# A fused attention and pooling block on one Trainium2 core: x^T laid out by the host, rows of x queued behind the weights, K's chain of round 0 two halves later

## The reference

```python
h = x * rsqrt(mean(x * x, axis=-1) + 1e-6) * norm_w
q, k, v, g_a, u_p, g_p = split(h @ w_in)              # six times 1024 columns
q, k = rope(rms_norm(q, q_norm_w)), rope(rms_norm(k, k_norm_w))   # by head of 64
a = softmax(q1 k1^T / 8) - lam * softmax(q2 k2^T / 8)  # 8 heads of 2 x 64
attn = rms_norm(a @ v) * subln_w * (1 - 0.2)
pool = (centred_mean(u_p, w) - u_p) @ w_pool * pool_scale   # w = 2, 4, 8, 16
out = x + concat(attn * silu(g_a), pool * silu(g_p)) @ w_out
```

## Time and profile before

| | us |
|---|---|
| median of 3 runs | 796.71 (796.64 to 797.11) |
| the profiled execution | 798.08 |
| its span, first to last instruction | 796.3 |
| PE busy | 780.4 (98%) |
| DVE busy | 550.3 (69%) |
| ACT busy | 389.6 (49%) |
| POOL busy | 31.3 (4%) |
| HBM read | 90.98 MB |
| mean granted TensorE clock | 1.000 |

### The profile page before, as it was taken

One profiled execution on the slowest core, in us unless ns is written; L12 is line 12 of the kernel. 1 busy time (PEld: TensorE's weight loads), 2 busy tenths in 40 slices (PEclk: granted clock), 3 DMA queues, 4 the chain that ended last, 5 costly groups with the idle time before them and its releaser, 6 DMA issues.

```text
span 796.3 us, 9964 instructions
## 1 busy us (share of the span) xinstructions
PE 780.4 (98%) x3522; PEld 643.5 (81%) x3522; DVE 550.3 (69%) x825; ACT 389.6 (49%) x647; POOL 31.3 (4%) x42
## 2 busy tenths in 40 slices
PE   6999999999999999999999999999999999999998
PEld 5888788888887888888878888887888878888886
DVE  3668775862786767637967674398667788777796
ACT  4945455444354644435436433544455556555552
POOL 0010000000000000000000000000000020233100
PEclk9999999999999999999999999999999999999999
DMA  9524521223244222232532123236222599999912
GB/s 319 170 81 133 158 80 54 80 79 106 85 130 132 78 80 79 75 111 85 144 113 79 53 79 97 88 105 182 79 64 72 164 246 296 327 250 211 196 54 105
DMA packets 69439, 101.87 MB, mean 128 GB/s; under 512 B 5152, under 2 KB 55584, under 8 KB 69408
## 3 DMA queue, kind: packets, MB, share of 16 engines
q1 hardware_dynamic: 62656, 82.52, 32.7%
q0 software_dynamic: 4736, 16.78, 10.8%
q10 hardware_dynamic: 2016, 2.18, 1.0%
HBM read 90.98 MB, written 4.19 MB: 120 GB/s over the span
## 4 chain that ended last, share of the span: by engine, by line
PE 81%; DVE 7%; ACT 5%; issue 3%; DMA 3%; SPq 0%; DVEq 0%; ACTq 0%
PE ps L410 78%; DMA q_stack<-v_hi 2%; PE ps L511 2%; ACT w_hi L620 1%; PE ps L403 1%; DVE v_hi L856 1%; DVE w_lo L820 1%; DMA mixed<-in_x 1%; ACT kh_twice L706 1%; DVE work L942 1%; DVE work L934 1%; DVE work L944 1%; DVE work L896 1%; ACT work L630 1%; ACT work L641 1%
## 5 line engine op out<-in xcount | busy, mean ns | idle before, releaser
L410 PE MATMUL ps<-h_hi,w_hi 128*128 128x512 f32 x768 | 303.5, 395 | 0.0
L410 PE MATMUL ps<-h_lo,w_hi 128*128 128x512 f32 x768 | 300.2, 391 | 0.0
L820 DVE TENSOR_TENSOR w_lo<-raw,w_hi 128x512 fp32r<-128x512 f32 x192 | 131.1, 688 | 144.7 <-ACT w_hi L620 142.7
L620 ACT CAST w_hi<-raw 128x512 fp32r<-128x512 f32 x192 | 117.4, 621 | 228.2 <-PE ps L410 226.5
L410 PE MATMUL ps<-h_hi,w_lo 128*128 128x512 f32 x768 | 205.6, 389 | 0.0
L410 PEld LDWEIGHTS ps<-h_hi,w_lo 128*128 128x128 f32 x768 | 144.4, 188 | 30.3
L410 PEld LDWEIGHTS ps<-h_lo,w_hi 128*128 128x128 f32 x768 | 144.9, 189 | 29.6 <-issue 0.2
L410 PEld LDWEIGHTS ps<-h_hi,w_hi 128*128 128x128 f32 x768 | 144.8, 189 | 29.4 <-issue 0.2
L410 PE MATMUL ps<-w_hi,h_hi 128*128 128x512 f32 x224 | 87.2, 389 | 0.4 <-DVE w_lo L841 0.4
L410 PE MATMUL ps<-w_lo,h_hi 128*128 128x512 f32 x224 | 87.2, 389 | 0.0
L410 PE MATMUL ps<-w_hi,h_lo 128*128 128x512 f32 x224 | 87.1, 389 | 0.0
(11 more groups left out here) (134 smaller groups left out, 800.0 us busy)
## 6 DMA issues: line engine op xcount, KB each, us to landing
raw<-in_w_in SPq DMA_DIRECT2D x96, 512.0 KB, 3.6
tall<-in_w_out SPq DMA_DIRECT2D x16, 512.0 KB, 11.0
raw<-in_w_out POOLq DMA_DIRECT2D x12, 512.0 KB, 11.3
wide_b<-in_w_out POOLq DMA_DIRECT2D x12, 512.0 KB, 14.5
tall<-in_w_out POOLq DMA_DIRECT2D x8, 512.0 KB, 13.6
mixed<-in_x SPq DMA_DIRECT2D x3, 1024.0 KB, 11.5
kh_twice<-kh_twice SPq DMA_DIRECT2D x8, 256.0 KB, 5.3
kl_twice<-kl_twice SPq DMA_DIRECT2D x8, 256.0 KB, 6.0
```

Of the source, the lines that this page charges most:

```text
L410: last = nc.tensor.matmul(dst, lhs, rhs, start=first and i == 0, stop=final and i == len(pairs) - 1, skip_group_check=True)
L620: nc.scalar.copy(w_hi[:, h % W_SLOTS, :], raw[:, unit % RAW_SLOTS, part * 512:part * 512 + 512]).then_inc(w_hi_ready, 1)
L820: nc.vector.tensor_tensor(w_lo[:, h % W_SLOTS, :], raw[:, unit % RAW_SLOTS, part * 512:part * 512 + 512], w_hi[:, h % W_SLOTS, :].bitcast( ...
```

## The change

1. The host passes x^T as a further input, `x_cols`. The five early pieces now bring k tiles of x^T into `mixed` (`x_turned`); x_high and x_low read them from SBUF. The transposes are gone. The fourth piece is followed by weight unit 2, the last by unit 3.
2. The rows of x, 1 MB per tile of 128 rows, are loaded a second time (`load_x_row`), into the space of q_stack, kh_twice, kl_twice, v_hi and v_lo: tiles 0 and 1 behind weight unit 5, tiles 2 and 3 behind unit 6. SP's round 0 is written out for that.
3. x_stats moves from steps 1 to 4 to steps 7 to 10, ahead of the step's weight cast. x_rms is now Exp(-0.5 Ln(.)), and x_rstd gets a refinement step on DVE of five tiny operations. The preload of the Sqrt table is gone.
4. In round 0 alone, K's steps 10 to 16 become 12 to 17 (the copies stay at 17 and 18), and the eps product moves from half 7 to half 11.

```diff
         def _(sp):
             def load_x_cols(n, a, b):
-                sp.dma_start(x_rows[:, :, a:b], x_tiles[:, :, a:b]).then_inc(x_in[n], 16)
+                sp.dma_start(x_turned[:, a:b, :], x_col_tiles[:, a:b, :]).then_inc(x_in[n], 16)
+            def load_x_row(t):
+                sp.dma_start(x_rows[:, t, :], x_tiles[:, t, :]).then_inc(x_row_in[t], 16)
...
-            load_x_cols(0, 0, 256)
+            load_x_cols(0, 0, 2)
             load_in(0, 0)
-            load_x_cols(1, 256, 512)
-            load_x_cols(2, 512, 1024)
+            load_x_cols(1, 2, 4)
+            load_x_cols(2, 4, 8)
             load_in(1, 0)
-            load_x_cols(3, 1024, 1536)
-            load_x_cols(4, 1536, 2048)
+            load_x_cols(3, 8, 12)
             load_in(2, 0)
+            load_x_cols(4, 12, 16)
             load_in(3, 0)
...
                     swap_halves(unit, r)
+                    if first and unit in (1, 2):
+                        load_x_row(2 * unit - 2)
+                        load_x_row(2 * unit - 1)
...
-            nc.scalar.preload_act_table(ACT.Sqrt)
...
             def x_high(q):
-                act.wait_ge(x_transposed, q + 1)
+                act.wait_ge(x_in[q if q < 2 else 1 + q // 2], 16)
...
-                    nc.scalar.activation(x_rms[:, :], x_ss[:, :], ACT.Sqrt, bias=eps_t[:, :],
-                                         scale=1.0 / D).then_inc(x_rms_ready, 1)
+                    nc.scalar.activation(x_rms[:, :], x_ss[:, :], ACT.Ln, bias=eps_t[:, :],
+                                         scale=1.0 / D).then_inc(x_logged, 1)
+                    act.wait_ge(x_logged, 1)
+                    nc.scalar.activation(x_rms[:, :], x_rms[:, :], ACT.Exp, scale=-0.5).then_inc(x_rms_ready, 1)
...
+                k_sums = 12 if first else 10
...
+                    if first and 7 <= m <= 10:
+                        x_stats(m - 7)
                     if last_round and m + 3 >= HALVES:
                         split_form_w(m + 3 - HALVES)
                     else:
                         split_high(m + 3, r)
-                    if first and m <= 4:
-                        x_stats(m - 1)
...
+                k_turn = 16 if first else 15
...
-                    if m in (15, 20):
+                    if m in (k_turn, 20):
                         chain(nc.vector.tensor_tensor(wk(1), wk(1), twice(sin_t), ALU.mult))
```

More of the change, by code:

```diff
@@ L199, in hybrid_block @@
         x_in = [sem(f"x_in{i}") for i in range(5)]
+        x_row_in = [sem(f"x_row_in{i}") for i in range(ST)]
         rstd_squared = sem("rstd_squared")
@@ L308, in swap_halves, with sp_round @@
                     sp.dma_start(kl_twice[0:64, 1].bitcast(F32), kl_twice[64:128, 1].bitcast(F32)).then_inc(k_moved, 16)
-            with sp.Fori(0, ROUNDS - 1) as r:
+            def sp_round(r, first=False):
                 for unit in range(UNITS):
@@ L319, in _ @@
                     swap_halves(unit, r)
+                    if first and unit in (1, 2):
+                        load_x_row(2 * unit - 2)
+                        load_x_row(2 * unit - 1)
+            sp_round(0, first=True)
+            with sp.Fori(1, ROUNDS - 1) as r:
+                sp_round(r)
             r = ROUNDS - 1
@@ L390, in _ @@
         def _(pe):
[L392 to L405, removed]
             def products(dst, pairs, first, final):
@@ L416, in pe_round @@
                     g, hk = divmod(m, G_HALVES)
[L417 to L424, removed]
                     if first and g == K:
@@ L458, in pe_round @@
                     last.then_inc(w_used, 1)
-                    if first and m == 7:
+                    if first and m == 11:
                         pe.wait_ge(eps_diag_ready, ST)
@@ L476, in pe_round @@
                     if m == 25:
+                        if first:
+                            pe.wait_ge(ident_in, 16)
                         pe.wait_ge(evacuated, r * 4 + 1 + START)
@@ L591, in x_high @@
             def x_high(q):
-                act.wait_ge(x_transposed, q + 1)
+                act.wait_ge(x_in[q if q < 2 else 1 + q // 2], 16)
                 for kk in range(2):
                     k = 2 * q + kk
-                    nc.scalar.activation(h_hi[:, k, :], ps[:, 2 + 2 * (q % 3) + kk, :], ACT.Copy,
+                    nc.scalar.activation(h_hi[:, k, :], x_turned[:, k, :], ACT.Copy,
                                          scale=nw[:, k:k + 1]).then_inc(h_hi_ready, 1)
@@ L600, in x_stats @@
                     act.wait_ge(x_squared, t)
-                else:
-                    for n in range(5):
-                        act.wait_ge(x_in[n], 16)
+                act.wait_ge(x_row_in[t], 16)
                 nc.scalar.activation(at_hi[:, :, :].rearrange("p t n -> p (t n)"), x_rows[:, t, :], ACT.Square,
@@ L684, in act_round @@
                         if first and n == 0:
+                            act.wait_ge(x_squared, 1)
                             act.wait_ge(lam_summed, 1)
@@ L812, in x_low @@
                     ins = nc.vector.scalar_tensor_tensor(
-                        out=h_lo[:, k, :], in0=ps[:, 2 + 2 * (q % 3) + kk, :], scalar=nw[:, k:k + 1],
+                        out=h_lo[:, k, :], in0=x_turned[:, k, :], scalar=nw[:, k:k + 1],
                         in1=h_hi[:, k, :].bitcast(F32), op0=ALU.mult, op1=ALU.subtract)
@@ L873, in dve_round @@
                         setup(nc.vector.memset(ones_all_r[:, :].bitcast(F32), 1.0))
-                    if first and m == 6:
+                    if first and m == 11:
                         dve.wait_ge(x_squared, ST)
@@ L880, in dve_round @@
                                                     None, ALU.mult).then_inc(eps_diag_ready, 1)
[L881 to L884, removed]
+                    if first and m == 12:
                         dve.wait_ge(eps_spread, 1)
@@ L887, in dve_round @@
                         dve.wait_ge(eps_row_ready, 1)
+                    if first and m == 13:
+                        dve.wait_ge(x_rms_ready, 1)
+                        setup(nc.vector.tensor_scalar(x_eps[:, :], x_eps[:, :], -0.5 / (HEAD_DIM * EPS), None, ALU.mult))
+                        setup(nc.vector.tensor_tensor(x_rstd[:, :], x_rms[:, :], x_rms[:, :], ALU.mult))
+                        setup(nc.vector.tensor_tensor(x_rstd[:, :], x_rstd[:, :], x_eps[:, :], ALU.mult))
+                        setup(nc.vector.tensor_scalar(x_rstd[:, :], x_rstd[:, :], 1.5, None, ALU.add))
+                        nc.vector.tensor_tensor(x_rstd[:, :], x_rstd[:, :], x_rms[:, :], ALU.mult
+                                                ).then_inc(x_rstd_ready, 1)
                     if m == 18:
                         qk_low(0, 0)
-                    if m in (10, 18):
+                    if m in (k_sums, 18):
                         n = int(m == 18)
```

22 lines of the change are left out of this document (12 added, 10 removed).

## The result

| | before | changed |
|---|---|---|
| median of the runs | 796.72 us (796.64 to 797.11) | 803.61 us (803.14 to 803.81) |
| profiled execution | 798.08 us, span 796.3 | 803.46 us, span 801.7 |
| mean granted clock | 1.000 | 0.997 |

The ratio is 1.0075, 95% interval 1.0063 to 1.0087: slower by 6.9 us in the medians, by 5.4 us between the two profiled executions. The prediction said 801.4 us, with 804.3 as its upper end.

A forecast was written before the change was run, and what follows sets the result against it. Bound: Q's move in round 0, fed by PE's work and K's and Q's chain. PE: -5.6 + 3.4 + 1.6 + 6.4 - 1.1 = +4.7 us, giving 802.8 profiled, median 801.4 us; range 797.3 to 804.3.

The forecast's parts named there:

- What bounds: In round 0, the end of Q's move, 89.27 us before the change, sets the whole kernel's time; nothing touched lies behind it.
- PE's own work: Start of round 0: transposes gone, first product at 9.7 us, half 7 ends at 33.5; PE gains 5.6 us.
- The rows of x: Row 0 lands at 32.2 us, x_stats follows, sq_lo ends at 42.4; PE waits 3.4 us before K's sum.
- rival 1: The rows are no obstacle: 798.0 us, within 0.2% of no change; chance 0.13.
- The eps product, K's chain: Eps diagonal covered by 0.8 us, half 12 at 49.6; K normed 12.5 us later, at 62.1; PE waits 1.6 us.
- Q's chain: From K normed to the end of Q's move 31.9 us, ending at 94.0; PE waits 6.4 us in pieces.
- The sum: PE's gain and waits in round 0 added up to +4.7 us, 802.8 us for the profiled execution.
- From the profiled execution to the median: Whole kernel: the profiled execution stood 1.4 us above the median, so 802.8 us became a median of 801.4.
- (2): Faster: the 31.5 us from K normed to Q's move are partly waiting for PE; down to 790.0 us; chance 0.13.
- (3): The rows come later still, row 3 past 44 us, so the eps product waits too: 803 to 806 us; chance 0.14.

The follow-up runs named there:

- e3: The changed kernel with 14 unused products on PE before the wait for Q's move; 801.26 us, ratio 1.0046.
- e4: The changed kernel without the loads of x's rows, x_stats squaring tiles of x^T instead; 802.7 us, ratio 1.0067.
- f2: The changed kernel with the table of Ln and Exp loaded at the start; 810.82 us, ratio 1.0167.
- e2: The changed kernel with K's chain back in steps 10 to 16, eps product and diagonal left out, eps_row zero; 798.18 us, ratio 1.0005.
- h3: h2 with eight more unused products before each of the waits for K's squares and the eps diagonal; 797.28 us, ratio 1.0002.
- e1: The kernel before with only K's steps 10 to 16 made 12 to 17 and the eps product moved to half 11; 806.72 us, ratio 1.0111.
- f1: The changed kernel with early table load, rows queued ahead of constants, x_stats at steps 5 to 8, K's chain back, nothing left out; 799.26 us, ratio 1.0018.
- g3: f2 with the nine small constants issued by POOL instead of SP; 806.15 us, ratio 1.0105.
- h1: f1 with the nine small constants on POOL and weight unit 5 ahead of the last row tile; 798.62 us, ratio 1.0012.
- h2: h1 with nine unused products before the wait for Q's move in round 0; 797.68 us, ratio 1.0003.

## Why the prediction was right, and where not

- **What bounds**: right. Q's move is the one point whose delay carries to the end; nothing behind 100 us changed.
- **PE's own work**: 5.6 us forecast. Half 7 ended at 34.40, not 33.5, so it was 4.7 us. The table load was on the path as said, 6.46 to 7.74; the Trainium skill (ScalarE: Activation LUTs, What ACT_TABLE_LOAD costs) adds a drain of about 1.38 us, but h_hi follows 0.02 us behind the load, so the row decides. The first product came 0.36 us later than forecast, and the slow pace lasted to about 15.
- **The rows of x**: the term that was mis-sized. I forecast a wait of 3.4 us before K's squares; it was 0.85 us. PE came 0.9 us later, and sq_lo ended at 40.80, 1.6 us earlier than the 42.4 forecast, because row 0 landed at 29.3 instead of 32.2. The failing step was to take weight unit 4's issue and landing, 20.88 and 27.3, from the kernel before: the loads in front of it were issued faster, and it landed at 24.9. The rate that I took was not the fault, 4.3 us from unit 4 to row 0. What I held against rival 1 was right: the passes of x_stats stand between K's squares and the casts wherever the rows are, and left 0.85 us of wait.
- **The eps product, K's chain**: right. Covered, half 12 at 48.38 (49.6), then exactly 12.5 us to K normed, and a wait of 1.6 us for it.
- **Q's chain**: 32.1 us against 31.9. Q's move ended at 92.96 against 94.0: 1.2 us earlier from half 12, 0.2 us later in the chain behind it.
- **What is missing**: the lower clock behind the wait, 1.6 us, shown by e3. I named a wait of over 3 us for that place and did not ask what PE's clock does behind it.
- **The sum**: +4.7 forecast, +3.7 and +1.6 measured between the profiled executions. It is nearly right by luck: two errors of opposite sign, 1.0 and 1.6, met.
- **From the profiled execution to the median**: I took 1.4 us off, because the profiled execution of before stood that far above its median. That of the changed kernel stood 0.15 below its own. This is 1.5 of the 2.2 us by which 801.4 missed 803.61. No trace shows what made the one execution of before longer than its median; the pace at the start, below, is one thing that differs between executions.
- **Rivals**: (1) was right about the rows in this kernel (e4) and wrong about the time, since the 12.5 and 32 us behind half 12 hold either way. (2) was shut out: the distance from half 12 to Q's move was 44.6 us, 44.4 forecast. (3) did not happen here. f2 is a case near it: row 0 5.6 us later cost another 7 us, but PE waited for K's squares and not for the eps product.

## What to carry to other kernels

When two strings of work run side by side to one meeting point, take work off the one that ends last; e2 and h3 had 64 transposes less on the other and were no faster. Before you move a chain two steps later, count the distance from it to the point that others wait for: two halves, 5.5 us on PE, put Q's move 6.0 us later (e1). And where the new schedule leaves TensorE a wait of 2 us or more, look at the granted clock behind it: where it fell at Q's move, that cost 1.6 to 2.6 us, and a few unused products in the gap avoided it (e3, h3). When you carry a landing over from the old trace, carry the issue time over only if the same issues stand in front of it.

## What was not expected of the hardware

- Which waits bring the granted clock down isn't told by their length alone. It fell in or behind waits for Q's move of 3.5 us (changed kernel, f2), 3.7 (e1), 3.4 (e4) and 2.4 (f1), waits for K's squares of 6.8 (f2) and 3.7 (g3), and pairs of waits with little work between them, 1.5 and 2.2 (h1), 2.4 and 2.2 (h2). It did not behind 2.1 (e2), 1.7 (h1), 2.2 for the eps diagonal in f1, or 3.5 for Q's move in g3, where 16 products took 3.93 us. The Trainium skill (TensorE: Matmul & The Clock Gate, Part 1) says that the gate goes by how busy the array has been of late; the falls agree, and for the 3.5 us in g3 no run here shows a reason.
- In f2 the DMA traffic was low for about three microseconds (123, 10 and 73 GB/s from 21 to 24 us), and this made 7 us in the end: one row tile landed 5.6 us later, and ACT's order handed that on. The one edit is a table load 4.7 us earlier on another engine; how it leads to the low traffic isn't shown.
- The pace of the first products, 0.43 us apart, changes to 0.23 at another time in each execution: near 12.4 us in e1, 13.5 in e4, 15 in the changed kernel and 16 in e2. The profile gives a granted clock of 1.00 all the while, so no row here names the cause. Worked out from these times and paces, it moves PE's work by up to 1.7 us (an estimate).
- SP's queue, with ACT's beside it at first, moved up to 414 GB/s over 4 us. The Trainium skill (DMA: Bandwidth & Descriptors, Where 436 GB/s comes from) gives about 358 GB/s as the limit that binds for loads from HBM, and quotes 425 for one large measured transfer; the 414 here lie above the first and near the second, so the measurement decides against the first for this program, which ran on one core alone.
